# One attention layer and ConvFFN step: query projections packed for two head pairs, rotary rows saved and multiplied later, plain rows split from PSUM

## The reference, cut to what matters

```python
c_q = rms_norm(d[..., :384], g_q_norm)                  # 1056 tokens x 384
q = (c_q @ w_a_uq).reshape(b, t, 16, 96)                # 16 heads, 64 plain + 32 rotary columns
q_nope = q[..., :64]
q_rope = apply_rope(q[..., 64:], cos, sin)              # x1*cos - x2*sin, x1*sin + x2*cos
sc = (einsum(q_nope, k_nope) + einsum(q_rope, k_r)) * ATTN_SCALE
sc = where(k_pos <= q_pos, sc, -inf); p = softmax(sc); o = einsum(p, v)
```

## Time and profile before

| | |
|---|---|
| median of three runs | 1625.86 us (1623.02 to 1628.99) |
| the profiled execution | 1623.65 us |
| its span, first to last instruction | 1621.8 us |
| mean granted clock of PE | 0.997 of full |
| DVE, instructions | 934.8 us busy, 1818 |
| ACT, instructions | 586.7 us busy, 1281 |
| first exp of the first pair, of the second | 114.19, 163.79 us |
| DMA | 109.18 MB, 67 GB/s |

### The profile page before, as it was taken

One profiled execution on the slowest core, in us unless ns is written; L12 is line 12 of the kernel. 1 busy time (PEld: TensorE's weight loads), 2 busy tenths in 40 slices (PEclk: granted clock), 3 DMA queues, 4 the chain that ended last, 5 costly groups with the idle time before them and its releaser, 6 DMA issues. The chain is left out here.

```text
span 1621.8 us, 29612 instructions
## 1 busy us (share of the span) xinstructions
PE 1585.6 (98%) x10341; PEld 1404.9 (87%) x10341; DVE 934.8 (58%) x1818; ACT 586.7 (36%) x1281; POOL 189.3 (12%) x293
## 2 busy tenths in 40 slices
PE   7989999999998999999999999999999999999998
PEld 6988878888786666667889999999999999999996
DVE  4665666656664565555766455645545554465547
ACT  5455655556553333332233131221312213131136
POOL 1000000000000430000003021120211202021100
PEclk9999999999999999999999999999999999999999
DMA  6111111011113765533114020220102112020103
GB/s 208 58 29 31 29 24 24 14 28 24 18 59 107 234 208 172 171 119 95 39 44 126 27 65 13 65 65 26 55 23 65 40 37 65 26 65 13 40 27 118
DMA packets 150967, 109.18 MB, mean 67 GB/s; under 512 B 54623, under 2 KB 139805, under 8 KB 150736
## 3 DMA queue, kind: packets, MB, share of 16 engines
q1 hardware_dynamic: 148704, 102.17, 21.5%
q0 software_dynamic: 1584, 5.19, 1.1%
q10 hardware_dynamic: 576, 0.52, 0.1%
HBM read 101.88 MB, written 10.14 MB: 69 GB/s over the span
## 5 line engine op out<-in xcount | busy, mean ns | idle before, releaser
L1925 PE MATMUL banks<-act_hi,up_hi 128*128 128x352 f32 (+2 forms) x1040 | 335.5, 323 | 0.7 <-PEq L1497 0.7
L1926 PE MATMUL banks<-act_lo,up_hi 128*128 128x352 f32 (+2 forms) x1040 | 335.1, 322 | 0.0
L1927 PE MATMUL banks<-act_hi,up_lo 128*128 128x352 f32 (+2 forms) x1040 | 334.9, 322 | 0.0
L1925 PEld LDWEIGHTS banks<-act_hi,up_hi 128*128 128x128 f32 x1040 | 195.5, 188 | 1.0 <-issue 0.9
L1926 PEld LDWEIGHTS banks<-act_lo,up_hi 128*128 128x128 f32 x1040 | 195.3, 188 | 0.0
L1927 PEld LDWEIGHTS banks<-act_hi,up_lo 128*128 128x128 f32 x1040 | 195.2, 188 | 0.0
L2228 DVE TENSOR_TENSOR o_t<-o_t,banks 128x352 f32<-128x352 f32 x240 | 120.9, 520 | 94.3 <-PE banks L1927 94.0
L2207 DVE SCALAR_TENSOR_TENSOR conv_out<-conv_in,conv_now,conv_out 128x1072 f32<-128x1072 f32 x42 | 64.5, 1536 | 185.4 <-ACT conv_out L2081 185.4
L1018 DVE TENSOR_REDUCE neg_max<-banks 128x1 f32<-128x896 f32 (+7 forms) x128 | 96.7, 756 | 116.8 <-PE banks L804 116.3
L2072 ACT ACTIVATE conv_in<-banks 128x352 f32<-128x352 f32 x84 | 36.3, 457 | 336.1 <-PE banks L1927 336.1
L1925 PE MATMUL banks<-gated_hi,down_hi 128*128 128x352 f32 x480 | 155.8, 325 | 0.0
(11 more groups left out here) (338 smaller groups left out, 3080.8 us busy)
## 6 DMA issues: line engine op xcount, KB each, us to landing
weight_stage<-in_w_f_up SPq DMA_DIRECT2D x44, 512.0 KB, 4.6
c_stage<-in_cache_kv_latent SPq DMA_DIRECT2D x140, 128.0 KB, 2.3
down_stage<-in_w_f_down SPq DMA_DIRECT2D x22, 512.0 KB, 4.3
head_weights_stage<-in_cache_kv_latent SPq DMA_DIRECT2D x56, 128.0 KB, 2.2
rope_query_tab<-in_cache_kv_latent SPq DMA_DIRECT2D x56, 128.0 KB, 2.2
o_t<-in_x_prompt SPq DMA_DIRECT2D x8, 512.0 KB, 3.7
rope_rows<-in_cache_k_rope SPq DMA_DIRECT2D x256, 16.0 KB, 2.0
wo_stage<-in_w_a_out POOLq DMA_DIRECT2D x8, 512.0 KB, 4.6
```

Source lines behind the costliest of these rows:

```text
L1925: nc.tensor.matmul(o, ws[0], xs[0], start=first, stop=False)
L1926: nc.tensor.matmul(o, ws[0], xs[1], start=False, stop=False)
L1927: return nc.tensor.matmul(o, ws[1], xs[0], start=False, stop=last)
```

## The change

Of every even pair p, "rotary units" r0, r1, r2 compute the 32 rotary columns of four heads, two of pair p and two of pair p + 1, in 128 columns. Every pair has "plain units" n0, n1, n2 with the 64 plain columns of both its heads. Odd pairs have no rotary units. The swapped columns are gone: the weights are no longer swapped, the key's second copy of its rotary rows is stored with halves exchanged instead, and the table has 32 rows of cosines and of sines, four times repeated.

- ACT copies a rotary bank to `raw` (`rope_saved`). DVE multiplies it later by cosines and sines, in operations of 32 partitions (`rotate`, two per head and chunk), into `q_rotary`. From there ACT makes the high halves (`rope_hi`, two copies) and DVE the low ones (`rope_lo`, two).
- A plain bank is split from PSUM: ACT writes the scaled high halves (`nope_hi`, two), DVE the low ones by one three-operand operation for each head (`nope_lo`, two).
- `NEXT_AT` becomes two tables, for an even and an odd next pair, and `ROTATE_AT` and others give the steps of the rest. v1 is now the last unit of a stage, and the banks change hands otherwise.
- The first scores of a pair wait for k0's halves; the second for the low halves of n0. In the first pair, DVE does nope_lo, rotate and rope_lo of chunks 2 and 1 before the first row maximum, and rotates chunk 0 between the first and the second.
- Odd pairs split only half of the query weights. An even pair's weights come by 8 transfers, an odd pair's by 4, where there were 5.
- For decode, PE multiplies the swapped part of `m.qr` by a permutation in step 4 of the last pair, and DVE adds (`rope_blocks`, four operations) in step 5. POOL's additions are gone.
- `vt` lies in unused columns of `probs_t`.

```diff
-    s2 = np.concatenate([-sin, sin], 1).T * np.float32(ATTN_SCALE)
-    plain = np.full((NOPE, TOK), ATTN_SCALE, np.float32)
-    query = np.stack([np.concatenate([plain, c2, s2], 0), np.concatenate([c2, s2, plain], 0)], 1)
+    s2 = np.concatenate([sin, -sin], 1).T * np.float32(ATTN_SCALE)
+    query = np.stack([np.tile(c2, (4, 1)), np.tile(s2, (4, 1))], 1)
...
-                for at in (DOWN - ROPE, DOWN):
-                    nc.vector.tensor_tensor(nrm[0:r, b, at:at + 16], rt[0:r, 0, :], rt[0:r, 1, :], ALU.subtract)
-                    last = nc.vector.tensor_tensor(nrm[0:r, b, at + 16:at + 32], rt[0:r, 2, :], rt[0:r, 3, :], ALU.add)
+                for at, swapped in ((DOWN - ROPE, 0), (DOWN, 16)):
+                    nc.vector.tensor_tensor(nrm[0:r, b, at + swapped:at + swapped + 16], rt[0:r, 0, :], rt[0:r, 1, :], ALU.subtract)
+                    last = nc.vector.tensor_tensor(nrm[0:r, b, at + 16 - swapped:at + 32 - swapped], rt[0:r, 2, :], rt[0:r, 3, :], ALU.add)
...
+        for h in range(2):
+            c = (2 * p + h) * QK_HEAD
+            sp.dma_start(self.q_staged[:, :, 0, h * NOPE:(h + 1) * NOPE], wq[:, :, c:c + NOPE]).then_inc(self.staged, 16)
+        for h in range(0 if p % 2 else 4):
+            c = (2 * p + h) * QK_HEAD + NOPE
+            sp.dma_start(self.q_staged[:, :, 1, h * ROPE:(h + 1) * ROPE], wq[:, :, c:c + ROPE]).then_inc(self.staged, 16)
...
+CHUNKS = "210"
+N_CHUNKS = len(CHUNKS)
+EARLY = [["wt", "r2", "r1", "r0", "k1", "n2", "v0", "n1", "k0", "n0", "v1"], ["wt", "v0", "k1", "n2", "n1", "k0", "n0", "v1"]]
+OWN = ["t0", "t1", "ql"]
+FIRST = ["v0", "k0", "r0", "n0", "wt", "v1", "k1", "r2", "n2", "r1", "n1"]
+LOWS = [["n0", "r2", "n2", "n1", "r1", "r0"], ["r2", "n2", "r1", "n1", "n0", "r0"]]
...
-NEXT_AT = {4: "wt", 5: "v0", 6: "v1", 8: "k1", 9: "q02", 10: "q12", 11: "q01", 12: "q11", 14: "k0", 15: "q00", 16: "q10"}
+NEXT_AT = [{4: "wt", 5: "r2", 6: "r1", 8: "r0", 9: "k1", 10: "n2", 11: "v0", 12: "n1", 14: "k0", 15: "n0", 16: "v1"},
+           {4: "wt", 6: "v0", 9: "k1", 10: "n2", 12: "n1", 14: "k0", 15: "n0", 16: "v1"}]
+ROTATE_AT = [{6: ("2", 0), 7: ("2", 1), 8: ("1", 0), 9: ("1", 1), 10: ("0", 0), 11: ("0", 1)},
+             {3: ("2", 0), 4: ("2", 1), 5: ("1", 0), 6: ("1", 1), 7: ("0", 0), 8: ("0", 1)}]
+ROPE_HI_AT, ROPE_LO_AT = {9: "2", 12: "1"}, {10: "2", 13: "1"}
+NOPE_HI_AT, NOPE_LO_AT = {11: "2", 13: "1", 16: "0"}, {12: "2", 14: "1", 16: "0"}
+K_LO_AT = {10: "k1", 15: "k0"}
+SWAP_AT = 4
 INV_AT = {7: 3, 10: 2, 13: 1}
-BANK = {"q02": 1, "q12": 3, "q01": 1, "q11": 3, "k0": 1, "q00": 3}
-BEFORE = {"q01": "q02", "q11": "q12", "k0": "q01", "q00": "q11", "t1": "t0", "ql": "t1", "v0": "wt", "v1": "v0"}
+BANK = {"k1": 3, "n2": 1, "n1": 3, "k0": 1, "n0": 3}
+BEFORE = {"t0": "v1", "t1": "t0", "ql": "t1", "r2": "wt", "r1": "r2", "n1": "k1", "k0": "n2", "n0": "n1"}
...
+                if n == 0 and p:
+                    bank_free(p, "k0")
+                if n == 0 and p == 0:
+                    bank_free(p, "k1")
+                if n == 1:
+                    bank_free(p, "n0" if p else "r2")
                 if n % 4 == 0 and g >= 1:
-                    pe.wait_ge(ql_ok, p * len(Q_UNITS) + (2 * (4 - g) if p else min(6, 2 * (5 - g))))
+                    pe.wait_ge(ql_ok, 2 * N_CHUNKS * p + (2 * (4 - g) if p else {3: 3, 2: 5, 1: 6}[g]))
...
+            def swapped_rope():
+
+                bank_free(PAIRS - 1, "ql")
+                pe.wait_ge(zr, 1)
+                pe.wait_ge(rh_ok, rope_count(PAIRS - 1, "2"))
+                nc.tensor.matmul(ps[0:ROPE, 7, :], m.swap, m.qr[:, 1, :, :].rearrange("r b c -> r (b c)"),
+                                 start=True, stop=True).then_inc(sw_ps, 1)
...
+            def rope_saved(p, c):
+
+                act.wait_ge(pj, pj_count(p, "r" + c))
+                act.wait_ge(rp_ok, N_CHUNKS * p)
+                copy(raw[:, CH * int(c):CH * int(c) + CH], ps[:, proj_bank(p, "r" + c), 0:CH]).then_inc(pj_act, 1)
+
+            def rope_hi(p, c):
+
+                cols = slice(CH * int(c), CH * int(c) + CH)
+                act.wait_ge(rp_ok, rope_count(p, c))
+                if c == "2":
+                    for hh in range(2):
+                        for part in range(2):
+                            r0 = (NOPE, 0)[hh] + part * ROPE
+                            copy(m.qr[:, part, :, (2 * p + hh) * DEC_SEQ:(2 * p + hh + 1) * DEC_SEQ],
+                                 qf[r0:r0 + ROPE, SEQ:TOK].rearrange("p (b t) -> p b t", t=DEC_SEQ))
+                copy(q_hi[NOPE:P, 0, cols], qf[NOPE:P, cols])
+                copy(q_hi[0:NOPE, 1, cols], qf[0:NOPE, cols]).then_inc(rh_ok, 1)
+
+            def nope_hi(p, c):
+
+                cols, bank = slice(CH * int(c), CH * int(c) + CH), proj_bank(p, "n" + c)
+                act.wait_ge(pj, pj_count(p, "n" + c))
+                for hh in range(2):
+                    r = slice(hh * NOPE, (hh + 1) * NOPE)
+                    last = nc.scalar.activation(q_hi[r, hh, cols], ps[r, bank, 0:CH], ACT.Copy, scale=ATTN_SCALE)
+                last.then_inc(nh_ok, 1)
+                if c == "2":
                     at = SEQ - 2 * CH
-                    for part in range(2):
-                        r0 = (NOPE, 0)[hh] + part * ROPE
-                        copy(m.qr[0:ROPE, part, :, (2 * p + hh) * DEC_SEQ:(2 * p + hh + 1) * DEC_SEQ],
-                             qf[r0:r0 + ROPE, i, at:CH].rearrange("p (b t) -> p b t", t=DEC_SEQ))
-                    rows_ = slice(hh * NOPE, (hh + 1) * NOPE)
-                    last = copy(qn[rows_, hh * N_SAMPLE:(hh + 1) * N_SAMPLE], qf[rows_, i, at:CH])
-                    if hh:
-                        last.then_inc(qn_ok, 1)
-                copy(q_hi[:, hh, c:c + CH], qf[:, i, :]).then_inc(qh_ok, 1)
+                    for hh in range(2):
+                        r = slice(hh * NOPE, (hh + 1) * NOPE)
+                        last = nc.scalar.activation(qn[r, hh * N_SAMPLE:(hh + 1) * N_SAMPLE], ps[r, bank, at:CH], ACT.Copy, scale=ATTN_SCALE)
+                    last.then_inc(qn_ok, 1)
...
+            for name in FIRST:
+                if name[0] == "k":
+                    k_hi(0, name)
+                elif name[0] == "r":
+                    rope_saved(0, name[1])
+                elif name[0] == "n":
+                    nope_hi(0, name[1])
+                    if name[1] != "0":
+                        rope_hi(0, name[1])
...
+                    if n == 0:
+                        rope_hi(p, "0")
...
+                    unit = NEXT_AT[(p + 1) % 2].get(n, "") if more else ""
+                    if more and n in NOPE_HI_AT:
+                        nope_hi(p + 1, NOPE_HI_AT[n])
+                    if more and n in ROPE_HI_AT:
+                        rope_hi(p + 1, ROPE_HI_AT[n])
+                    if unit in ("wt", "v0", "v1"):
+                        take(p + 1, unit)
+                    if unit in ("r2", "r1", "r0"):
+                        rope_saved(p + 1, unit[1])
+                    if unit in ("k0", "k1"):
+                        k_hi(p + 1, unit)
...
-            def q_scale(p, name):
-                i, at = place_in(p, name, Q_UNITS), p * len(Q_UNITS) + place_in(p, name, Q_UNITS)
-                dve.wait_ge(pj, pj_count(p, name))
-                if at >= 2:
-                    dve.wait_ge(ql_ok, at - 1)
-                nc.vector.tensor_tensor(qf[:, i % 2, :], ps[:, proj_bank(p, name), 0:CH],
-                                        tab[:, int(name[1]), int(name[2]) * CH:int(name[2]) * CH + CH], ALU.mult).then_inc(pj_dve, 1)
-
-            def q_low(p, name):
-                i, hh, c = place_in(p, name, Q_UNITS), int(name[1]), int(name[2]) * CH
-                dve.wait_ge(qh_ok, p * len(Q_UNITS) + i + 1)
-                nc.vector.tensor_tensor(q_lo[:, hh, c:c + CH], qf[:, i % 2, :], f32(q_hi[:, hh, c:c + CH]), sub).then_inc(ql_ok, 1)
+            def rotate(p, c, hh):
+
+                cols = slice(CH * int(c), CH * int(c) + CH)
+                dve.wait_ge(pj_act, act_count(p - p % 2, "r" + c))
+                if p:
+                    dve.wait_ge(ql_ok, count_in(lows, p - 1, "r" + c))
+                at = NOPE * (p % 2) + hh * ROPE
+                for part in range(2):
+                    to = (NOPE, 0)[hh] + part * ROPE
+                    last = nc.vector.tensor_tensor(qf[to:to + ROPE, cols], raw[at:at + ROPE, cols], tab[at:at + ROPE, part, cols], ALU.mult)
+                if hh:
+                    last.then_inc(rp_ok, 1)
+
+            def rope_lo(p, c):
+                dve.wait_ge(rh_ok, rope_count(p, c))
+                cols = slice(CH * int(c), CH * int(c) + CH)
+                nc.vector.tensor_tensor(q_lo[NOPE:P, 0, cols], qf[NOPE:P, cols], f32(q_hi[NOPE:P, 0, cols]), sub)
+                nc.vector.tensor_tensor(q_lo[0:NOPE, 1, cols], qf[0:NOPE, cols], f32(q_hi[0:NOPE, 1, cols]), sub).then_inc(ql_ok, 1)
+
+            def nope_lo(p, c):
+                dve.wait_ge(nh_ok, nope_count(p, c))
```

(35 more changed lines are left out.)

220 lines of the change are left out of this document (97 added, 123 removed).

## The result

The changed kernel takes 1634.66 us (median of 5 runs, 1634.25 to 1636.52), the kernel before 1625.95 us (5 runs): a ratio of 1.0053, interval 1.0042 to 1.0063. That is 8.7 us slower, where 8.5 us faster was forecast. The profiled execution after took 1634.25 us (span 1632.4), beside the 1623.65 us (1621.8) of before; so the two traces differ by 10.6 us and the medians by 8.7. The kernel before was measured again beside every group of experiments, with medians from 1625.9 to 1626.95 us, so a difference of under 1 us between experiments of different groups tells nothing.

A forecast was written before the change was run, and what follows sets the result against it. TensorE was taken to bound attention. Terms -14.8 (short stages), -0.5 (long stages), +6.8 (start) and 0 (last pair) sum to -8.5 us: 1615.2 from the profiled execution, 1617.4 on the median; 8-in-10 range 1608.5 to 1625.

The forecast's parts named there:

- the four short stages: Stages of pairs 0, 2, 4, 6, which project an odd pair: each 3.7 us shorter, together 14.8 us.
- the three long ones: Stages of pairs 1, 3, 5, which project an even pair: each 0.17 us shorter, together 0.5 us.
- short stages over 49 us: Stated sign of error: stages projecting an odd pair were forecast near 46.9 us; over 49 would prove the forecast wrong.
- 1, packed columns: Projections: 9 units instead of 12 for two pairs, 18.0 us less on TensorE, 4.5 a short stage.
- 2, the end of a pair: The 0.87 us wait before the next pair's first scores goes, worth 6.1 us over seven pairs.
- 3, what the loop gives back: Attention loop: added VectorE and ScalarE work costs 1.7 us a short stage and 0.7 a long one.
- Items 8 and 11 have no filler any more: Short stages: remark in the item-by-item count that these items lose their projection units; no size given.
- at item 13: Long stages: 0.25 us late at this item, part of the 0.7 given back.
- 4, the start: First pair: uncovered VectorE work delays item 3's scores by 6.35 us, plus 0.45 for slow clock: +6.8 us.
- The hole ahead of item 2's scores: First pair: TensorE idle from 116.6 to 120.2 us, stated as a sign of over 3 us.
- 5, the last pair: GpSimd's additions go; one TensorE matmul and four VectorE additions come: net 0, give or take 1 us.
- Rival C: VectorE's order bounds from about 44 us a pair: short stages stay 50.5, long grow 1; 1636 us, chance 0.08.

The follow-up runs named there:

- e15: Changed kernel with e4, e5, first head weights loaded later; short-stage rotations in items 4 to 7, chunk 0's in the next stage's items 0 and 1: 1616.81 us.
- e4: Changed kernel with VectorE's inverse (reciprocal and spread) right behind the row maximum, ahead of the low halves, in every item: 1627.70 us.
- e1: Changed kernel with one rotation of the short stages (head 1 of chunk 0) moved from item 8 to item 11: 1630.65 us.
- e13: Changed kernel with e4, e5, first head weights loaded later, and the short-stage rotation places of e14: 1624.89 us.
- e7: Changed kernel with each rotary multiplication 8 columns wide instead of 352, leaving that computation out, waits and order kept: 1622.47 us.
- e5: Changed kernel with rotary chunk 0's high and low halves moved to items 4 and 5, and the start's first row maximum ahead of chunk 1's rotation: 1630.91 us.
- e12: Changed kernel with nine unread matmuls at the end of the last pair, 4 ahead of its last values, 5 behind its last transposes: 1632.16 us.
- e14: Changed kernel with the short stages' rotations in items 5, 6, 7, 9, 10, 11 instead of 3 to 8: 1636.48 us.
- e8: Kernel before the change with the inverse ahead of VectorE's projection work in every item, as in e4: 1625.16 us, ratio 0.9996.
- e10: e12's nine unread matmuls added to the changed kernel with e1, e4, e5 and later first head weights (1621.06 us without them): 1621.60 us.
- e6: Changed kernel with unread matmuls: ten ahead of the very first scores, and 4, 6 and 4 at the end of the last pair: 1636.23 us.

## Why the prediction was wrong, step by step

Between the forecast's -8.5 us and the traces' +10.6 lie 19.1 us. Counting the start up to the scores of item 3, where the forecast counted it, the four short stages miss 10.0 of them (-14.8 forecast, -4.8 measured), the three long ones 3.5 (-0.5, +3.0), the start 1.8 (+6.8, +8.55), the last pair 0.5 and the start of decode 3.3. The forecast's own sign of being wrong came too: short stages over 49 us.

- **1, packed columns: 18 us off TensorE.** Right in matmuls (106 fewer in the records), and e15 shows the 4.5 us a short stage can be had. In the change a short stage got only 1.3 us shorter.
- **2, the end of a pair: -6.1.** Right: the wait is gone, and the steps 15-0 and 0-1 together fell from 10.52 to 9.50 us. In the long stages that is so only behind the long step 14-15; where this is mended (e4), the two take 10.2 us.
- **3, what the loop gives back: this step failed.** Short stages were to give back 1.7 us and gave back 4.1 (4.5 + 0.87 - 1.3). The forecast said "Items 8 and 11 have no filler any more". It looked at the units taken from TensorE and not at the rotation that stands in item 8: missed whole, 1.2 to 1.7 us in step 10-11 (e1). Step 6-7 lost 0.9 us where 0.4 was forecast (3.72 us in e13 to e15, 4.58 after); the chain at items 12 to 14 lost 1.3 (e4: 0.53 and 0.76) where 1.0 was; steps 1-2 and 2-3, beside chunk 0's conversions, lost 0.5 in every stage behind the first where 0.2 was. Long stages were to give back 0.7 and gave back 1.9; 1.2 of it is step 14-15, from 0.67 to 1.88 us, as e4 and e7 each show, where 0.25 stood "at item 13". The rotation of item 11, the low half of item 12 and then the inverse stand there in one queue, and I had added up VectorE's 38 us (39.6 measured) against 50, as if a sum could say it.
- **4, the start: +6.8.** Too small by 1.8 us. The first exp came 7.0 us late, but that is near 6.8 by chance: the forecast had it at 119.0, 4.8 late, and it began at 121.19; 1.44 us of the difference is the first part of this execution. The hole ahead of item 2's scores was 1.2 us and not over 3, as the matmuls ahead of it ran at the lower clock and filled the rest. The chain itself, scores, maximum, exp:

```profile
114.83 0.77 PE L763 MATMUL banks<-k_hi,q_hi 128*128 128x512 f32 x1 [3.40 <-DVE q_lo L1104]
...
118.98 0.52 DVE L1094 TENSOR_TENSOR q_lo<-q_rotary,q_hi 64x352 fp32r<-64x352 f32 x1 [1.07 <-ACT q_hi L939]
...
120.06 1.09 DVE L1126 TENSOR_REDUCE neg_max<-banks 128x1 f32<-128x896 f32 x1
...
121.19 1.01 ACT L949 ACTIVATE probs<-banks,neg_max 128x896 f32<-128x896 f32 x1 [0.94 <-DVE neg_max L1126]
...
125.95 0.50 PE L763 MATMUL banks<-k_hi,q_hi 128*128 128x512 f32 x1 [1.29 <-ACT probs L949]
```

  Item 3's scores start at 125.95, +8.55 where +6.35 and 0.45 for the clock were forecast; e5 shows 1.3 us of it to be order alone.
- **5, the last pair: 0.** +0.5, within its bounds.
- **Not in the sum:** the half clock at the start of decode, a term that the forecast didn't have, 3.3 us in the trace; e12 gets 2.5 of it.
- **The base.** The profiled execution of before is at the lower end of its kind: clock 0.997, 1623.65 us. Among the runs of that kernel beside the experiments, from 1623.28 to 1630.98 us, the longer ones have the lower clock (23 beside the first four: 0.997 at 1623.28, 0.992 at 1630.17). The forecast had moved its sum to the median, rightly.
- **Rival C named the mechanism, VectorE's order,** but asked for 44 us of it before it would decide. It decided at 39.6 us, in part: short stages gained 1.3 us instead of nothing, long ones grew by the 1.0 us it gave. Its 1636 us lie nearest to the measured 1634.66; its chance of 0.08 was too small. Its measure fails as well: e15 has 41.9 us of VectorE in a long stage, and TensorE busy all through a short one beside 37.6.
- **The port.** The forecast weighed the Trainium skill's rule in "SBUF — State Buffer" on the shared port pair. The low half at 112.43 ran beside GpSimd's casts and took 0.64 us instead of 0.52; the rule's whole wait isn't seen.

```profile
112.30 0.39 POOL L581 CAST wv_hi<-head_weights_stage 128x256 fp32r<-128x256 f32 x1
112.43 0.64 DVE L1094 TENSOR_TENSOR q_lo<-q_rotary,q_hi 64x352 fp32r<-64x352 f32 x1 [2.02 <-ACT q_hi L939]
```

## What to carry to other kernels

When work moves from a full engine to one that is 60% busy, its sum doesn't settle it: write down, for each place where an operation is put into an in-order queue, the next instruction behind it that another engine waits for, and put it where there is none within its length. Here the same multiplications cost 2 us a stage more or less by their item numbers alone (e1 against e14), clock included; e15, with two of them moved to the next stage, takes 1.4 us less than e13 for a short and a long stage together. Take the short hand-over (here a reciprocal and its spread, 0.4 us) ahead of the long work in every item: it cost nothing where it didn't matter (e8) and saved 7 us where it did (e4).

## What the runs showed of the hardware

- A multiplication over 32 partitions and 352 columns takes 517 ns, one over 128 partitions took 514, a subtraction over 64 partitions and 512 columns 695: VectorE's time went by columns and not by partitions. Packing four heads' rotary columns left a unit at nine matmuls on TensorE and doubled VectorE's operations on the queries from 12 to 24 a pair.
- A wait that holds TensorE 1.5 us longer can cost as much again in clock: the ends of e14's short stages went through 6 us at 0.72 behind it. Behind e13's shorter hold (step 14-15 at 2.07 us instead of 2.93) the clock fell at one of four.
- Filling a hole with unread matmuls kept the clock at 1.00 wherever it was tried at the end of attention, but lowered the median only once in three (e12 -2.5 us; e10 +0.5; e6, with six of them in the way of the last transposes and ten at the start, +1.6).
